# 8 KB transfers and groups in twos in the expert layer of a decoder trunk

## The chip, the cores and the metric

One core of a Trainium2 chip runs the whole program. The metric is the device time of one execution in microseconds (us). TensorE (PE) multiplies matrices into PSUM accumulators, PEld is its weight load, VectorE (DVE) and ScalarE (ACT) do elementwise work, GpSimd (POOL) issues the gathers through index lists, and SyncE (SP) issues the transfers of weights from HBM, which 16 DMA engines carry out.

## The reference, cut to what matters

Two layers over 256 tokens of width 1024, float32. Layer 0 is windowed attention and a dense SwiGLU, layer 1 a Mamba-2 mixer and eight experts, of which each token takes two. The change touches the expert part alone:

```python
logits = (h @ w_router)
top_vals, top_idx = lax.top_k(logits, 2)
top_w = jax.nn.softmax(top_vals, axis=-1)
combine = sum(one_hot(top_idx, 8) * top_w[..., None], axis=-2)
out = 0
for e in range(8):
    g, u = split(h @ w_gu[e], 2)            # w_gu[e]: 1024 x 7168
    out = out + combine[..., e:e + 1] * ((silu(g) * u) @ w_down[e])   # w_down[e]: 3584 x 1024
```

The weights of the eight experts are 352 MB, and all of them are read once.

## The kernel before, in words

A weight tile is 128 rows by 1024 columns (512 KB, 4 KB in each partition). A large matrix product is done in three parts: ScalarE writes a rounded copy of the tile (w_hi, `split_hi`), VectorE the remainder (w_lo, `split_lo`), and TensorE multiplies high by high, high by low and low by high (L2600, L2601, L2608 in `weight_tile`). There are four places each for w_hi and w_lo (SPLIT), so ScalarE can be four tiles ahead of TensorE.

An expert has 84 tiles: seven groups of columns of w_gu, eight tiles (k) each, and 28 tiles of w_down. Groups 0, 2, 4 are gates, group 1 is half gate and half up, 3, 5, 6 are up (`MIX_COLS`, `MIX_UP`). The experts are sorted by their number of tokens and dealt out in pairs: the even one, `p`, has 128 slots and uses the three-part product; the odd one has 64 slots and is multiplied in plain float32 straight from the landed tile (L3097 in `small_step`, no split). `pair_order` writes out the order of tiles (`MOE_SEQ`): in the first pair (r = 0) 16 tiles of the large expert run ahead and then small and large units take turns; in later pairs all 84 large tiles come first and then all 84 small ones.

A large group fills one of two accumulators `acc[0]`, `acc[1]` of 128x1024, in turn (`Body.pair`: `(q + r) % 2` with q = j % 2); the small expert's groups fill the halves of `acc[2]`, and its output goes to the accumulator r % 2. TensorE waits in `open_pair` until the accumulator was emptied. The emptying is `mix_gates` (ScalarE, Silu) and `mix_products` (VectorE), and for an expert's output `output` (VectorE: `yw` or `y_s`, L2026). VectorE and ScalarE run through `MOE_SEQ` in a fixed order: at each tile first the split of that tile, then what `DUE` holds for it. A group's emptying is due three tiles after its last one, an expert's output three tiles after its last.

SP goes through `MOE_LOADS`. 30 tiles of expert 0 are loaded early, into places that come free in the layer before (`FIRST_MOE`, `FIRST_TILES`, `home_free`). Then SP waits for `order_ready`, which says which expert is next, and loads the rest in the order of `MOE_SEQ` into 20 places (12 of `raw` and 8 others, `STAYS`); each load waits until the former tile there was used (L821). Routing is done on VectorE: `positions`, then at given tiles of expert 0 `order_of_experts` (step 4), `second_expert` (6), `rows_of_slots` (18), `places_of_tokens` (21), `positions_of_tokens` (23).

Of the kernel before, what the change touches and what calls it, by code (L numbers as in the profile page):

```python
# [15 lines left out]
P = 128  # L16
# [24 lines left out]
RAW = 12  # L41
# [16 lines left out]
LARGE_AHEAD = 2  # L58
# [34 lines left out]
def build(nc, A, out, square_in, table_in, overflow_at=P):  # L93
# [305 lines left out]

    def units(p):  # L400
        steps = [KD] * FJ + [FK // 4] * 4
        return [[(p, n) for n in range(sum(steps[:u]), sum(steps[:u + 1]))] for u in range(len(steps))]

    def pair_order(r):
# [4 lines left out]
        for u, later in enumerate(small_):  # L409
# [3 lines left out]
    FIRST_MOE = ("row_b", 4, "more0", "more1", "mod5", "mod0", "once0", "once1", "once2", "once3", 5, 6, 7, "mod1",  # L413
                 "once4", "once5", "once6", "once7", 8, 9, 10, 11, 12, 13, 14, 15, "mod2", "mod3", "mod4", "rest8")
    FIRST_TILES = ("row_b", 4, "more0", "more1", "mod5", 5, 6, 7, 8, 9, 10, 11, 12, 13, 14, 15, "once0", "once3", "once7",
                   "mod2", "mod3", "mod4", "rest8", "once4", "once1", "once5", "once2", "once6", "mod0", "mod1")
    ONLY_ONCE = ("mod0", "mod1") + tuple(f"once{n}" for n in range(8))
    STAYS = ("row_b", "more0", "more1", "mod5", "mod2", "mod3", "mod4", "rest8")
    assert len(ONLY_ONCE) == RAW_ONCE and len(STAYS) == RAW_EXTRA
    raw_homes = {n: raw[:, n, :] for n in range(RAW)}  # L420
# [5 lines left out]
    def home_of(what):  # L426
        return (raw0["wout"] + what) % RAW if isinstance(what, int) else RAW + (STAYS + ONLY_ONCE).index(what)
# [5 lines left out]
    SECOND_FROM = len(FIRST_MOE)  # L433
    MOE_LOADS = [(0, FIRST_TILES.index(home)) for home in FIRST_MOE]
    MOE_LOADS += [tile for tile in MOE_SEQ if tile not in MOE_LOADS]
    raw_home, raw_turn, raw_before, turns, held = {}, {}, {}, {}, {}

    def keep_in(no, home):
        turns[home] = turns.get(home, 0) + 1
        raw_home[no], raw_turn[no], raw_before[no] = home, turns[home], held.get(home)  # L440
        held[home] = no

    for no in range(raw0["moe"]):
        keep_in(no, no % RAW)
    free = []
    for m, (p, n) in enumerate(MOE_LOADS):
        no = raw0["moe"] + MOE_AT[p, n]
        if m < len(FIRST_MOE):
            keep_in(no, home_of(FIRST_MOE[m]))
            if FIRST_MOE[m] not in ONLY_ONCE:  # L450
                free.append(raw_home[no])
        else:
            keep_in(no, min(free, key=lambda home: held[home]))
    for n in range(BODY):
        keep_in(raw0["moe"] + EXPERTS * BODY + n, n % RAW)
# [4 lines left out]
    def raw_landed(no):  # L460
        return raw_ready[raw_home[no]], 16 * raw_turn[no]
# [18 lines left out]
    SMALL_SLOT_AT = (35, 51, 59, 61)  # L480
    ORDER_AT, SECOND_AT, SLOTS_AT, PLACES_AT, POS_AT = 4, 6, 18, 21, 23
# [3 lines left out]
    def body_pieces(mixture):  # L485
        after = {}
        for j in range(FJ):
            if mixture:
                gi = MIX_GROUP[j]
                after.setdefault(KD * (gi + 1) + 3 + 2 * MIX_UP[gi].index(j), []).append(("h", j, 0))  # L490
            else:
                after.setdefault(KD * (j + 1) + 3, []).extend(("h", j, t) for t in range(T))
        if mixture:
            for n in range(len(G_BLOCKS)):
                after.setdefault(FJ * KD + 8 + 4 * n, []).append(("gather", n))
# [20 lines left out]
    def round_pieces():  # L516

        n = len(G_BLOCKS)
        for p, step_ in MOE_SEQ:
            found = []  # L520
            if p % 2 == 0:
# [5 lines left out]
                if step_ == (KD * LARGE_AHEAD - 1 if p == 0 else FJ * KD + 8):  # L527
                    found.append(("picked",) if p == 0 else ("small",))
            else:
# [5 lines left out]
                found += [("gather", g) for g in range(len(G_BLOCKS) if p < STORED else 0) if step_ == FJ * KD + 8 + 4 * g]  # L535
# [14 lines left out]
    def events_of_round():  # L550

        due = {}
        for m, (p, step_) in enumerate(MOE_SEQ):
            if step_ < FJ * KD and step_ % KD == KD - 1:
                due.setdefault(m + 3, []).append(("group", p, step_ // KD))
# [157 lines left out]
    class Body:  # L713
# [26 lines left out]
        def pair(self, j, t):  # L740
# [4 lines left out]
            if not self.rnd:  # L745
# [3 lines left out]
                q = (1 if j == FJ else j) % 2  # L749
                return (q + r) % 2, before_pair((q + r) % 2, r) + (3 if j == FJ else j // 2)  # L750
            q = 2 if j == FJ else j % 2
            return q, self.used[q] + (0 if j == FJ else j // 2) + rep(self.e, moe_uses[q])

        def half(self, j):

            return j % 2, self.p // 2 * (4, 3)[j % 2] + j // 2

        def full(self, j):

            return self.spl + KD * (j + 1) + rep(self.e, BODY)  # L760
# [5 lines left out]
    def small_rows(j):  # L766
        return acc[2][:, j % 2 * HALF:(j % 2 + 1) * HALF]
# [28 lines left out]
    def mixture_source(w_gu, w_down, s):  # L796
        if s < FJ * KD:
            gi, k = divmod(s, KD)
            return w_gu[k * P:(k + 1) * P, MIX_COLS[gi]:MIX_COLS[gi] + TW]
        k = s - FJ * KD  # L800
        return w_down[k * P:(k + 1) * P, :]

    block = nc.Block()
    with block:
# [3 lines left out]
        def _(sp):  # L808
            def load(no, src):

                before = raw_before[no]
# [6 lines left out]
                dst = raw_tile(no)  # L818
                if len(src.shape) == 3:
                    dst = dst.rearrange("p (h n) -> p h n", h=src.shape[1])  # L820
                sp.dma_start(dst, src).then_inc(raw_ready[raw_home[no]], 16)  # L821
# [90 lines left out]
            def home_free(m):  # L912

                if m == 0:
                    sp.wait_ge(w_used, spl0["wout"] + 4)
                elif m == 2:
# [3 lines left out]
                elif FIRST_MOE[m] == "mod1":  # L920
                    sp.wait_ge(w_used, spl0["wout"] + 8)
                elif FIRST_MOE[m] == "once4":
                    sp.wait_ge(xb_full, y_piece(3, 1) + 1)
                elif FIRST_MOE[m] == "mod2":
                    sp.wait_ge(gated, gated_no("wout", 2 * KD - 1))
                elif FIRST_MOE[m] == "mod3":
                    sp.wait_ge(hm_rest, 4 * T)
                    sp.wait_ge(hm_rows, T)
                elif FIRST_MOE[m] == "rest8":
# [2449 lines left out]
```

## Time and profile before

| | us |
|---|---|
| median of 3 runs (1513.43 to 1515.9) | 1515.46 |
| the profiled execution, its own time | 1516.27 |
| its span, first to last instruction | 1514.5 |
| TensorE busy | 1463.6 (97%) |
| VectorE busy | 988.8 (65%) |
| ScalarE busy | 746.2 (49%) |
| mean transfer rate over the span | 331 GB/s |
| mean granted TensorE clock | 0.996 |

The span is 1.8 us shorter than the execution's own time. Busy time of TensorE is modelled at its ends, so that 97% is not a statement on its peak. The expert layer begins at 643 us and takes more than half of the time.

### The profile page before, as it was taken

Reading aid. Unit: us, or ns where it says so; the run is one execution under the profiler, and the core shown is the slowest. Engines: PE = TensorE matmul, PEld = TensorE weight load, DVE = VectorE, ACT = ScalarE, POOL = GpSimd, SP = SyncE. Lnnn points to the kernel's source line nnn. Section 1 sums busy time; section 2 is a strip of 40 time slices with the busy share of each in tenths; the row PEclk is TensorE's granted clock in tenths of the full one; section 3 lists DMA queues with packets and bytes.
Section 4 is the critical chain, followed back from the end, with each engine's and each line's share of the span. In section 5 each row is a group of like instructions: output and inputs, shape, how many; then the busy total and the mean of one; then the engine's idle time right before and its main releaser. Section 6 shows DMA issues by size and latency. Waiting matters only on the chain.

```text
span 1514.5 us, 19554 instructions
## 1 busy us (share of the span) xinstructions
PE 1463.6 (97%) x6964; PEld 978.7 (65%) x6964; DVE 988.8 (65%) x1258; ACT 746.2 (49%) x977; POOL 13.8 (1%) x18
## 2 busy tenths in 40 slices
PE   7989999999999999899999999999999998999996
PEld 2836788788789888676666578632678531778431
DVE  2578788888668989776665689611789410989311
ACT  3574544444366876455544577500677300877200
POOL 0000000000000000001000000000000000000000
PEclk9999999999999999999999999999999999999999
DMA  9878698888265337688999999999999999999996
GB/s 363 320 272 287 250 392 308 295 287 305 68 228 167 98 101 262 249 308 329 410 409 409 401 409 408 372 411 400 409 409 409 409 409 399 409 409 408 392 409 266
DMA packets 156947, 501.90 MB, mean 331 GB/s; under 512 B 18483, under 2 KB 21196, under 8 KB 156840
## 3 DMA queue, kind: packets, MB, share of 16 engines
q1 hardware_dynamic: 155560, 496.53, 86.3%
q0 software_dynamic: 1280, 4.01, 0.8%
q8 instruction: 58, 0.95, 0.3%
q14 instruction: 49, 0.40, 0.1%
HBM read 498.33 MB, written 2.29 MB: 331 GB/s over the span
## 4 chain that ended last, share of the span: by engine, by line
PE 83%; DMA 6%; DVE 4%; SPq 3%; ACT 2%; issue 1%; DVEq 0%; ACTq 0%
PE acc L2600 18%; PE acc L2608 17%; PE acc L2601 17%; PE acc L3097 14%; SPq L821 3%; DMA raw<-in_moe_w_down 2%; DVE w_lo L1517 1%; PE xb L2986 1%; PE acc L2749 1%; PE xb L3027 1%; DMA raw<-in_moe_w_gu 1%; DMA raw_more<-in_moe_w_gu 1%; DMA mod<-in_moe_w_down 1%; PE xb L2648 1%; PE acc L3221 1%
## 5 line engine op out<-in xcount | busy, mean ns | idle before, releaser
L1517 DVE TENSOR_TENSOR w_lo<-raw,w_hi 128x1024 fp32r<-128x1024 f32 x353 | 425.6, 1223 | 107.2 <-ACT w_hi L976 97.4
L976 ACT ACTIVATE w_hi<-raw 128x1024 fp32r<-128x1024 f32 x353 | 370.1, 1059 | 200.2 <-PE acc L2608 142.8
L2600 PE MATMUL acc<-w_hi,g_hi 128*128 128x512 f32 x448 | 179.1, 400 | 2.6 <-issue 2.6
L2601 PE MATMUL acc<-w_hi,g_lo 128*128 128x512 f32 x448 | 174.9, 390 | 0.0
L2600 PE MATMUL acc<-w_hi,a_hi 128*128 128x512 f32 x384 | 153.5, 400 | 0.8
L2601 PE MATMUL acc<-w_hi,a_lo 128*128 128x512 f32 x384 | 149.9, 390 | 0.0
L2608 PE MATMUL acc<-w_lo,g_hi 128*128 128x512 f32 x448 | 138.8, 391 | 1.7 <-DVE w_lo L1517 0.9
L3097 PE MATMUL acc<-raw,g_s 128*64 128x512 f32 x552 | 128.2, 597 | 0.0
L2608 PE MATMUL acc<-w_lo,a_hi 128*128 128x512 f32 x384 | 118.4, 390 | 0.0
L2600 PEld LDWEIGHTS acc<-w_hi,g_hi 128*128 128x128 f32 x448 | 84.1, 188 | 34.6 <-issue 15.2
L1517 DVE TENSOR_TENSOR w_lo<-mod,w_hi 128x1024 fp32r<-128x1024 f32 x68 | 82.3, 1222 | 27.0 <-ACT w_hi L976 24.3
L2608 PEld LDWEIGHTS acc<-w_lo,g_hi 128*128 128x128 f32 x448 | 83.7, 188 | 21.9 <-DVE w_lo L1517 3.9
L2601 PEld LDWEIGHTS acc<-w_hi,g_lo 128*128 128x128 f32 x448 | 84.2, 188 | 16.3
L976 ACT ACTIVATE w_hi<-mod 128x1024 fp32r<-128x1024 f32 x68 | 71.6, 1060 | 37.4 <-PE acc L2608 21.4
L3097 PEld LDWEIGHTS acc<-raw,g_s 128*64 128x64 f32 x552 | 37.4, 137 | 75.2 <-issue 74.9
L2600 PE MATMUL acc<-w_hi,e_hi 128*128 128x512 f32 x216 | 85.7, 397 | 0.0
L2600 PEld LDWEIGHTS acc<-w_hi,a_hi 128*128 128x128 f32 x384 | 72.1, 188 | 19.0 <-DVE h L1931 2.8
L2601 PE MATMUL acc<-w_hi,e_lo 128*128 128x512 f32 x216 | 84.2, 390 | 0.0
L2608 PEld LDWEIGHTS acc<-w_lo,a_hi 128*128 128x128 f32 x384 | 72.1, 188 | 15.6
L2601 PEld LDWEIGHTS acc<-w_hi,a_lo 128*128 128x128 f32 x384 | 72.2, 188 | 13.8
L3097 PE MATMUL acc<-raw,e_s 128*64 128x512 f32 x268 | 71.4, 631 | 9.2 <-DMA raw<-in_moe_w_down 8.7
L1975 DVE TENSOR_TENSOR gate<-gate,acc 64x512 f32<-64x512 f32 x28 | 19.2, 684 | 77.4 <-PE acc L3097 72.8
(408 smaller groups left out, 2126.9 us busy)
## 6 DMA issues: line engine op xcount, KB each, us to landing
raw<-in_moe_w_gu SPq DMA_DIRECT2D x263, 512.0 KB, 12.5
raw<-in_moe_w_down SPq DMA_DIRECT2D x135, 512.0 KB, 15.1
raw<-in_ada_w SPq DMA_DIRECT2D x96, 512.0 KB, 5.9
mod<-in_moe_w_gu SPq DMA_DIRECT2D x90, 512.0 KB, 12.8
raw<-in_ffn_w_gu SPq DMA_DIRECT2D x56, 512.0 KB, 5.9
raw_more<-in_moe_w_gu SPq DMA_DIRECT2D x44, 512.0 KB, 12.2
mod<-in_moe_w_down SPq DMA_DIRECT2D x42, 512.0 KB, 15.2
raw<-in_ssm_w_in SPq DMA_DIRECT2D x40, 512.0 KB, 4.7
```

The lines of the kernel that those rows point to most:

```text
L821: sp.dma_start(dst, src).then_inc(raw_ready[raw_home[no]], 16)
L976: act.activation(w_hi[:, w % SPLIT, :], raw_tile(no), ACT.Copy).then_inc(hi_ready, 1)
L1517: dve.tensor_tensor(w_lo[:, w % SPLIT, :], raw_tile(no), r32(w_hi[:, w % SPLIT, :]), ALU.subtract).then_inc(raw_used, 1)
L1975: ins = dve.tensor_tensor(hidden, hidden, small_rows(j)[part, :], ALU.mult)
L2600: pe.matmul(o, l_hi[:, k, rows_], hi[:, col:col + HALF], start=new, stop=False)
L2601: pe.matmul(o, l_lo[:, k, rows_], hi[:, col:col + HALF], start=False, stop=False)
L2608: mm = pe.matmul(o, l_hi[:, k, rows_], lo[:, col:col + HALF], start=False, stop=end)
L2648: mm = pe.transpose(b[:, m * P:(m + 1) * P], src(m), ident)
L2749: mm = pe.matmul(o[j:j + 32, 0:HALF], cond[:, k:k + 1].to_broadcast([P, 32]), raw_tile(no)[:, cols], start=k == 1, stop=k >= KD - 2, skip_ ...
L2986: mm = pe.transpose(b[:, m * P:(m + 1) * P], hidden[:, m * P:(m + 1) * P], ident)
L3027: mm = pe.matmul(b[:, :], put_w[0][:, t, :], yw[:, hf * HALF:(hf + 1) * HALF], start=True, stop=True)
L3097: mm = pe.matmul(rows_[at_:at_ + SMALL, :], lhs[:, k, :], raw_tile(no)[:, m * HALF:(m + 1) * HALF], start=k == 0, stop=last, skip_group_ch ...
```

## The change

Tiles of the expert layer are loaded two at a time by one transfer of 1 MB into two neighbouring places. Where it can be, each partition gets one contiguous run of 8 KB instead of 4. For w_gu that needs two groups whose columns are neighbours, so the groups run in twos: (0, 2), (1, 3), (4), (5, 6), and their tiles alternate; group 4 stays alone, with two rows of 4 KB. For w_down each partition takes two neighbouring rows, so that the order of the hidden columns changes with it (`block_of`: the transposes read every second column). The groups of a two need two accumulators at once. `LARGE_AHEAD` is 1 unit of 16 tiles instead of 2 of 8. `order_of_experts` is done on VectorE before most of the first low parts, cut into two functions; the weights of the tokens and the other routing steps are done later, where the first small tiles run. The table for Silu is loaded before the early splits of ScalarE. Pieces of work (transposes of hidden columns, gathers, slots) have new steps.

```diff
-LARGE_AHEAD = 2
+LARGE_AHEAD = 1
+    GROUP_TWOS = ((0, 2), (1, 3), (4,), (5, 6))
+    GROUP_OF = [(js[n % len(js)], n // len(js)) for js in GROUP_TWOS for n in range(len(js) * KD)]
+    GROUP_OF += [(FJ, k) for k in range(FK)]
+    GROUP_HALF = (0, 0, 1, 1, 0, 1, 0)
+    GROUP_USE = (0, 1, 0, 1, 2, 2, 3)
+    GROUPS_DUE = {GROUP_END[js[0]] + 2: js for js in GROUP_TWOS}
+    HIDDEN_AT = (35, 37, 39, 59, 61, 63, 65)
-        steps = [KD] * FJ + [FK // 4] * 4
+        steps = [2 * KD, 2 * KD, KD, 2 * KD] + ([KD, KD, KD - 2, KD - 2] if p % 2 else [FK // 2, FK // 2])
+    FIRST_LOADS = ((14, "row_b"), (0, "more0", "more1"), (16, "once0", "once1"), (18, "once2", "once3"), (2, 4, 5), (4, 6, 7), (28, "mod0", "mod1"),
+                   (26, "once4", "once5"), (20, "once6", "once7"), (6, 8, 9), (8, 10, 11), (10, 0, 1), (12, 2, 3),
+                   (22, "mod2", "mod3"), (24, "mod4", "mod5"), (15, "rest8"))
-    ORDER_AT, SECOND_AT, SLOTS_AT, PLACES_AT, POS_AT = 4, 6, 18, 21, 23
+    GATHERS_AT = {0: (68, 72, 76), 1: (64, 68, 72)}
+    ORDER_AT, SECOND_AT, SLOTS_AT, PLACES_AT, POS_AT = 19, 10, 17, 18, 19
...
                 r = self.p // 2
                 if self.p % 2:
                     return r % 2, before_pair(r % 2, r) + 4
-                q = (1 if j == FJ else j) % 2
-                return (q + r) % 2, before_pair((q + r) % 2, r) + (3 if j == FJ else j // 2)
+                q = 1 if j == FJ else GROUP_HALF[j]
+                return (q + r) % 2, before_pair((q + r) % 2, r) + (3 if j == FJ else GROUP_USE[j])
...
+    def block_of(m):
+        return slice(m // 2 * 2 * P + m % 2, (m // 2 + 1) * 2 * P, 2)
...
+                elif n < FJ * KD:
+                    gi, k = GROUP_OF[n]
+                    if GROUP_OF[n + 1][0] == gi:
+                        dst = two_tiles(homes[0])
+                        src = w_gu[k * P:(k + 2) * P, MIX_COLS[gi]:MIX_COLS[gi] + TW].rearrange("(h p) n -> p h n", h=2)
+                    else:
+                        dst = two_tiles(homes[0]).rearrange("p h n -> p (h n)")
+                        src = w_gu[k * P:(k + 1) * P, MIX_COLS[gi]:MIX_COLS[gi] + 2 * TW]
+                else:
+                    k = n - FJ * KD
+                    dst = two_tiles(homes[0]).rearrange("p h n -> p (h n)")
+                    src = w_down[k * P:(k + 2) * P, :].rearrange("(p h) n -> p (h n)", h=2)
+                sp.dma_start(dst, src).then_inc(raw_ready[homes[0]], 16)
...
-            early_hi("moe", MOE_BEFORE)
-
             warm(ACT.Silu)
+            early_hi("moe", MOE_BEFORE, 2)
...
             positions()
-            for n in range(len(G_BLOCKS)):
+            gathered_lo(pc0["moe"], 0, highs_moe + 1)
+            early_lo("moe", MOE_BEFORE, 2)
+            order_of_experts()
+            for n in range(1, len(G_BLOCKS)):
                 gathered_lo(pc0["moe"] + n, n, highs_moe + n + 1)
-                if n:
-                    early_lo("moe", n, 2 * n)
+                early_lo("moe", n + 1, n + 2)
             first_round()
```

## Rows read from the trace of the kernel before

**Rows 1.** The page: busy time; transfer rate in 40 slices, GB/s.
```profile
PE 1463.6 (97%) x6964; PEld 978.7 (65%) x6964; DVE 988.8 (65%) x1258; ACT 746.2 (49%) x977; POOL 13.8 (1%) x18
...
GB/s 363 320 272 287 250 392 308 295 287 305 68 228 167 98 101 262 249 308 329 410 409 409 401 409 408 372 411 400 409 409 409 409 409 399 409 409 408 392 409 266
```

**Rows 2.** Windows: length, busy us (instructions), clock, DMA share, GB/s.
```profile
643.00:975.20 332.20, 331.32 (x1488) 225.09 (x1486) 236.08 (x255) 190.97 (x202) 9.34 (x9) 1.00 0.98 386
...
1287.10:1412.30 125.20, 124.44 (x548) 98.44 (x548) 111.81 (x103) 94.04 (x95) 0.00 (x0) 1.00 1.03 409
975.20:1066.60 91.40, 86.86 (x373) 26.21 (x373) 11.47 (x20) 7.76 (x14) 0.91 (x1) 0.98 1.01 394
1191.90:1287.10 95.20, 88.64 (x374) 25.41 (x373) 11.49 (x20) 7.75 (x14) 0.91 (x1) 0.98 1.03 405
1412.30:1504.60 92.30, 86.04 (x365) 24.27 (x364) 9.94 (x17) 5.33 (x10) 0.00 (x0) 1.00 0.95 375
```

**Rows 3.** Timeline, TensorE, two tiles' starts: start us, us.
```profile
1405.48 0.39 PE L2600 MATMUL acc<-w_hi,e_hi 128*128 128x512 f32 x1
...
1406.84 0.39 PE L2600 MATMUL acc<-w_hi,e_hi 128*128 128x512 f32 x1
```

**Rows 4.** Windows, small expert's matmuls (L3097) alone.
```profile
975.20:1036.00 60.80, 54.70 (x246) 16.92 (x248) 1.00 1.00 392
```

**Rows 5.** Timeline of SP's issues in the projection.
```profile
413.71 12.33 SPq L821 DMA_DIRECT2D raw<-in_ssm_w_in  x9
```

**Rows 6.** Windows: the projection (2 KB) and the last small expert (4 KB).
```profile
420.00:424.00 4.00, 4.00 (x20) 3.27 (x19) 3.78 (x7) 3.63 (x5) 0.00 (x0) 1.00 1.06 392
424.00:428.00 4.00, 4.00 (x24) 3.34 (x23) 1.65 (x2) 0.91 (x1) 0.00 (x0) 1.00 1.06 388
1440.00:1455.00 15.00, 15.00 (x68) 4.99 (x68) 2.06 (x3) 1.20 (x2) 0.00 (x0) 1.00 1.03 410
1410.00:1425.00 15.00, 15.00 (x69) 5.85 (x69) 2.34 (x5) 1.37 (x3) 0.00 (x0) 1.00 0.95 364
```

**Rows 7.** Timeline, all engines, start of the expert layer.
```profile
637.40 1.99 ACT L976 ACTIVATE w_hi<-raw_more 128x1024 fp32r<-128x1024 f32 x2
...
639.41 1.28 ACT L990 ACT_TABLE_LOAD   x1
...
640.81 0.85 ACT L1313 ACTIVATE g_hi<-xb 128x512 fp32r<-128x512 f32 x2
...
641.50 1.02 DVE L2064 TENSOR_TENSOR g_lo<-xb,g_hi 128x512 fp32r<-128x512 f32 x2 [0.55 <-ACT g_hi L1313]
...
643.16 0.48 PE L2600 MATMUL acc<-w_hi,g_hi 128*128 128x512 f32 x1
...
649.62 0.36 SPq L821 DMA_DIRECT2D raw_row<-in_moe_w_gu  x1
```

**Rows 8.** Groups by line, 1287 to 1413: busy us, mean ns, idle before.
```profile
L1517 DVE TENSOR_TENSOR w_lo<-raw,w_hi 128x1024 fp32r<-128x1024 f32 x51 | 61.3, 1223 | 23.0 <-ACT w_hi L976 21.4
L976 ACT ACTIVATE w_hi<-raw 128x1024 fp32r<-128x1024 f32 x50 | 52.6, 1060 | 12.8 <-PE acc L2608 11.4 <-DMA raw<-in_moe_w_gu 1.3
...
L1211 ACT ACTIVATE gate_l<-acc 128x1024 f32<-128x1024 f32 x3 | 3.1, 1020 | 0.5 <-PE acc L2608 0.5
...
L2083 DVE TENSOR_TENSOR gate_l<-gate_l,acc 128x512 f32<-128x512 f32 x4 | 2.6, 680 | 0.0
...
L1214 ACT ACTIVATE gate_end<-acc 128x512 f32<-128x512 f32 x1 | 0.6, 600 | 0.3 <-PE acc L2608 0.3
```

**Rows 9.** Timeline, all engines, a turn from small to large.
```profile
1065.46 1.06 ACT L976 ACTIVATE w_hi<-mod 128x1024 fp32r<-128x1024 f32 x1 [14.79 <-DMA mod<-in_moe_w_gu]
...
1066.62 0.47 PE L2600 MATMUL acc<-w_hi,g_hi 128*128 128x512 f32 x1 [1.34 <-issue]
...
1070.26 1.41 DVE L2026 TENSOR_TENSOR y_s<-acc,mod 64x512 f32<-64x512 f32 x2
...
1072.98 0.50 PE L2608 MATMUL acc<-w_lo,g_hi 128*128 128x512 f32 x1 [0.73 <-DVE w_lo L1517]
```

More of the change, by code:

```diff
@@ L426, in home_of, with two_tiles @@
     def home_of(what):
-        return (raw0["wout"] + what) % RAW if isinstance(what, int) else RAW + (STAYS + ONLY_ONCE).index(what)
+        return what if isinstance(what, int) else RAW + (STAYS + ONLY_ONCE).index(what)
+    def two_tiles(a):
+        if a < RAW:
+            return raw[:, a:a + 2, :]
+        name = (STAYS + ONLY_ONCE)[a - RAW]
+        at_ = int(name[-1])
+        return (mod if name[:3] == "mod" else raw_more if name[:4] == "more" else raw_once)[:, at_:at_ + 2, :]
     MOE_SEQ = [tile for r in range(EXPERTS // 2) for tile in pair_order(r)]
@@ L432, in build @@
         natives.append(natives[-1] + p % 2)
[L433 to L453, printed above, removed]
+    raw_home, raw_sem, raw_turn, turns, held = {}, {}, {}, {}, {}
+    def keep_in(nos, homes):
+        before = max((held[home] for home in homes if home in held), default=None)
+        turns[homes[0]] = turns.get(homes[0], 0) + 1
+        for no, home in zip(nos, homes):
+            raw_home[no], raw_sem[no], raw_turn[no] = home, homes[0], turns[homes[0]]
+            held[home] = no
+        return before
@@ new lines, in build, with moe_load @@
+    raw_before = {no: keep_in([no], [no % RAW]) for no in range(raw0["moe"])}
+    MOE_LOADS = []
+    def moe_load(tiles, homes):
+        nos = [raw0["moe"] + MOE_AT[tile] for tile in tiles]
+        MOE_LOADS.append((tiles, nos, homes, keep_in(nos, homes)))
+    for n, *names in FIRST_LOADS:
+        moe_load([(0, n + m) for m in range(len(names))], [home_of(name) for name in names])
+    SECOND_FROM = len(MOE_LOADS)
+    FIRST_TILES = sum(len(names) for _, *names in FIRST_LOADS)
+    homes_of_two = [(n, n + 1) for n in range(0, RAW + RAW_EXTRA, 2)]
@@ L454, in build @@
+    for m, (p, n) in enumerate(MOE_SEQ):
+        if n % 2 == 0 and (p or n >= FIRST_TILES):
+            homes = min(homes_of_two, key=lambda two: max(held[two[0]], held[two[1]]))
+            if homes[0] == RAW:
+                for q in range(2):
+                    moe_load([(p, n + q)], [homes[q]])
+            else:
+                moe_load([(p, n), (p, n + 1)], list(homes))
     for n in range(BODY):
-        keep_in(raw0["moe"] + EXPERTS * BODY + n, n % RAW)
+        raw_before[raw0["moe"] + EXPERTS * BODY + n] = keep_in([raw0["moe"] + EXPERTS * BODY + n], [n % RAW])
@@ L494, in body_pieces @@
             for n in range(len(G_BLOCKS)):
-                after.setdefault(FJ * KD + 8 + 4 * n, []).append(("gather", n))
+                after.setdefault(GATHERS_AT[0][n], []).append(("gather", n))
         else:
@@ L534, in round_pieces @@
                     found.append(("add", p - 1, ADDS_AT[p > 1].index(step_)))
-                found += [("gather", g) for g in range(len(G_BLOCKS) if p < STORED else 0) if step_ == FJ * KD + 8 + 4 * g]
+                found += [("gather", g) for g in range(len(G_BLOCKS) if p < STORED else 0) if step_ == GATHERS_AT[1][g]]
             for what in found:
@@ L553, in events_of_round @@
         for m, (p, step_) in enumerate(MOE_SEQ):
-            if step_ < FJ * KD and step_ % KD == KD - 1:
-                due.setdefault(m + 3, []).append(("group", p, step_ // KD))
+            if step_ + 1 in GROUP_END.values() and step_ < FJ * KD:
+                j = GROUP_OF[step_][0]
+                at_ = next(at_ for at_, js in GROUPS_DUE.items() if j in js)
+                due.setdefault(m + at_ - step_, []).append(("group", p, j))
             if step_ == BODY - 1 and p < STORED:
@@ L1923, in body @@
                         split_lo(B.raw_no(s), B.spl + s, e)
+                    for gi in GROUPS_DUE.get(s, ()) if B.mixture else ():
+                        mix_products(B, gi)
                     j, k = divmod(s, KD)
-                    if 1 <= j <= FJ and k == 2:
-                        if B.mixture:
-                            mix_products(B, j - 1)
-                        for t in range(0 if B.mixture else T):
+                    if not B.mixture and 1 <= j <= FJ and k == 2:
+                        for t in range(T):
                             q, _ = B.pair(j - 1, t)
```

140 lines of the change are left out of this document (73 added, 67 removed).

## The prediction

> **What bounds the kernel now.** I read the page first: TensorE is busy for 97% of the span, and from about slice 19 of 40 on the transfers run at 409 GB/s [rows 1]. Both look full, so the page alone cannot say which one sets the end. The windows by stretch can [rows 2]. The expert layer is one large expert (128 slots, PE work 1.36 us a weight tile: two tile starts lie 1406.84 - 1405.48 apart [rows 3]) and one small expert (64 slots) in turn. Up to 975.2 us TensorE is never idle (331.3 of 332.2 us). Then come small 91.4, large about 125, small 95.2, large 125.2, small 92.3 us. In the large stretches TensorE works 124.4 of 125.2 us: they are set by TensorE. In the small stretches it idles 4.5, 6.6 and 6.3 us while the transfers run near their full rate: there the transfers decide. The small stretch's own floor is the start at 975.2 us, where 246 matmuls, 61.5 tiles, took 60.8 us out of full buffers [rows 4], so about 1.0 us a tile with its other work, 84 us in all. So faster transfers can shorten three stretches of some 92 us, by at most some 8 us each, and nothing else.
>
> **Transfers of 8 KB.** A tile is 524,288 bytes. At 410 GB/s (pieces of 4 KB) it takes 1.280 us; in the projection, where SP issues ssm_w_in in pieces of 2 KB, the queue runs as full and moves 392 and 388 GB/s [rows 5, 6]. With the latter, a piece takes one of the 16 engines 84.5 ns at 2 KB (2,048 x 16 / 388) and 159.8 ns at 4 KB, so 75.3 ns for 2 KB more; a straight line gives 310.4 ns for 8 KB, 422 GB/s. With 392 it is 420. I take 420, 1.248 us a tile, a gain of 0.032. Bounds: 409 (an 8 KB piece costs two of 4 KB) and 435 (the slope of 75.3 ns alone, the fixed part of 9 ns gone). The Trainium skill (DMA: Bandwidth & Descriptors, "Why small descriptors are slow (HBM only)") gives a fixed overhead of about 3 cycles a packet beside one cycle per 32 bytes: 262 cycles against 259 for 8 KB, 1.1%. By it the gain would be 0.014 us a tile and the small stretches would come out some 3 us worse in total than below; the trace's step from 2 to 4 KB is about twice what that rule gives, so I go by the rows.
>
> In a small stretch of the new kernel 20 tiles are there at its start, since the buffers fill in the large stretch before it. Counting tiles by GB/s x time, the old stretches moved 68.7, 73.5 and 66.0 tiles [rows 2]; the second was longer because its buffers weren't full at its start. In the new kernel I count 69.7 for the first two (one more, because the large expert starts on a pair) and 64 for the last. Group 4 stays at 4 KB, 8 tiles. 61.7 x 1.248 + 8 x 1.280 = 87.2 us. To this comes the restart of the queue: the first free buffer is now a pair, so two tiles of 0.9 us plus 1.6 us until data flow, 3.4 us. In all 90.6: -0.8 and -4.6 us. The last stretch: 64 tiles are 56 x 1.248 + 8 x 1.280 = 80.1, the restart 3.4, what its old time holds beside 66.0 tiles of 84.5 and 1.7 of queue idle at its start (15 x (1 - 364 / 410) [rows 6]) is 6.1, and 0.9 comes on top because the last two tiles come together and are worked off one after the other: 90.5, -1.8 us. **Small stretches -7.2 us.**
>
> **The start.** ScalarE does two splits (1.99 us) and the table load (1.28) before the gather's high part at 640.81; VectorE's low part at 641.50 waits for it [rows 7]. The change leaves one split there, and takes six VectorE operations of 0.2 us from ahead of positions. The first gather piece is ready from about 639.7, so the high part starts 1.1 us earlier, the third piece's transposes follow, and the first expert tile starts at 642 instead of 643.16: **-1.2 us**; this carries to 975.2, since TensorE doesn't wait in between. The order of the experts is ready at about 643, so SP goes on at 644 instead of 649.62. I cost this at nothing: TensorE has 30 tiles in store and needs none of these transfers; buffers come free only as it works (1.36 us a tile), and at 975 us the buffers are full either way. Its cover would be gone if the 16 small tiles at 669 us were late; they are loaded by 663. second_expert (four VectorE operations and two picks, 1 us) at tile 10 is due at 655 and needed at 664; rows, places and positions lie in VectorE's slack beside the first small tiles.
>
> **Groups in twos hold TensorE.** A large expert's accumulators are two. Before, eight tiles fill one while the other is emptied; now tiles alternate between both, and a new pair of groups opens both within two tiles. Three places:
>
> (1) At a tile 56 (down) the accumulator of group 5 is needed, whose last tile is 54. VectorE first does the low part of tile 57 (its high part needs tile 53 done), then two products of 0.68. From tile 53's end: 0.3 + 1.06 + 1.22 + 1.3 = 3.9 us; TensorE is there at 2.72: 1.1 us lost. At tile 32 group 1's accumulator waits for Silu 0.60, the low part of 33 and a product 0.68: 0.5 us. At 17 and 41 only a Silu of 1.02 stands in the way, under one tile's 1.36: nothing [rows 8]. 1.6 x 3 large stretches (in the first pair of experts small tiles lie between): **+4.8 us**.
>
> (2) The turn from small to large is what I think decides. The small expert's output sits in the accumulator that the next large expert's group 2 takes. The first group to take it was group 1, at tile 8; now it is group 2, at tile 1. VectorE empties it (y_s, 1.41 us) only after the low part of the third large tile: 1070.26, 3.6 us after TensorE's first tile [rows 9]. That cost nothing at tile 8. Now tile 1 waits for it: from the landing of the first pair, the third tile lands 2.5 us later, high 1.06 + 0.2, low 1.23, y_s 1.41: 6.5 us; TensorE wanted it at 2.7. Lost 3.8, less 0.7 that it lost there before anyway (it waited for a low part, the last of [rows 9]): 3.1 us at each of two turns. At the first turn, near 851 us, tiles are in store and VectorE's three low parts follow the last add, at small tile 80 (1.1 on TensorE, 0.7 on VectorE): 1.8 + 3 x 1.15 + 1.4 = 6.7 against 1.1 + 3 x 0.88 + 1.36 = 5.0: 1.7. **+7.9 us**, and the large stretches are TensorE's, so it isn't made good; the transfers only fill the buffers sooner.
>
> (3) In the small expert the same alternation stands behind transfers, so nothing.
>
> **Strided transposes** for the new row order: 28 x 4 per large expert of 0.1 us; between nothing and double, +3 us a stretch; the address step alone gives no reason, I take nothing.
>
> Sum: -7.2 - 1.2 + 4.8 + 7.9 = **+4.3 us** on the profiled 1516.27 (span 1514.5 and 1.8 around it): 1520.6. The median of the runs is 0.8 below the profiled one: 1519.8, +0.28%.
>
> **The rivals.** (a) Forecast, chance 0.50, own range 1515 to 1524 (the waits of (1) and (2) by a third either way). (b) TensorE isn't held: the accumulators come free in time, so 12.7 us fall away: 1507.1. For it: VectorE is busy only 112 of 125 us in a large stretch. Against: its order is fixed by program, and [rows 9] show it. It is faster than before by a measurable amount as soon as (1) and (2) together cost less than 5.3 us. Chance 0.22. (c) 8 KB pieces move no faster than 4 KB: 61.7 x 0.032 x 3 = 5.9 more, 1525.7. For it: no row shows a piece above 4 KB. Chance 0.14. The skill's page on DMA (section "SWDGE vs HWDGE vs iDMA") calls packets of up to 4096 B the preferred ones, which would go with this; nothing here shows it. (d) They move at 430: (1.248 - 1.219) x 61.7 x 3 = 5.4 less, 1514.4. Chance 0.14.
>
> About 0.2% (3 us) is what a measurement can tell from no change: 1512.4 and 1518.5. Faster: (b) 0.20, (d) 0.03, (a) 0.01: 0.24. Same: (a) 0.15, (d) 0.11, (b) 0.02: 0.28. Slower: (a) 0.34, (c) 0.14: 0.48. Range 1506 to 1527: from just below (b) to just above (c).
>
> **What would show it.** GB/s near 420 in small stretches (right), 409 (c). TensorE's second large tile starts 5 us after its first at two turns and the wait names y_s (2). Waits before tiles 32 and 56 in each large stretch, which grow from 125 to about 130 us. First expert tile at 642. Queue idle at all large stretches' ends. I am wrong if VectorE's y_s comes ahead of the third low part, or if a large stretch stays at 125 us.

## The result and the profile after

The changed kernel takes 1528.06 us (median of 4 runs, 1527.55 to 1529.39), the kernel before 1515.68 (1513.43 to 1516.59); the ratio is 1.0084, 95% interval 1.0072 to 1.0097. It is **slower by 12.4 us**, where 4.3 were forecast, and lies just above the range of 1506 to 1527. The profiled execution took 1529.39 us, its span is 1527.6; so the two profiles stand 13.1 us apart. No time below counts one execution, of the kernel with the gates later, that took 2441 us at a mean granted clock of 0.56.

The page of the changed kernel, against [rows 1]: busy time, transfer rate in 40 slices, and the number of transfer pieces.

```profile
PE 1464.9 (96%) x6964; PEld 989.8 (65%) x6964; DVE 990.2 (65%) x1258; ACT 745.4 (49%) x977; POOL 16.1 (1%) x18
...
GB/s 362 316 277 285 243 393 310 288 287 310 75 214 157 106 101 295 219 329 295 419 420 419 409 409 346 356 417 408 420 416 369 376 418 409 418 413 334 377 418 304
DMA packets 117017, 501.79 MB, mean 328 GB/s; under 512 B 13635, under 2 KB 16348, under 8 KB 81848
```

Work is the same (6964 matmuls), the rate has risen from 409 to 419 and 420 where the queue is full, and yet other slices fell to 334 to 377. These lie mostly where a large stretch ends: the buffers are full there and SP waits for one to come free (106 and 107 us in sum in the last two large stretches, 36 in the last one before). TensorE is busy in them (18.9 of 18.9 us from 1165.0 on, at 326 GB/s): it takes a tile every 1.36 us, less than the queue can bring. The windows by stretch, against [rows 2], cut at the first matmul of each kind (length, busy of TensorE, its weight loads, VectorE, ScalarE, GpSimd, granted clock, DMA share, GB/s):

```profile
669.96:685.54 15.58, 15.58 (x65) 4.89 (x65) 4.51 (x15) 2.43 (x3) 0.00 (x0) 0.89 0.70 269
685.54:711.49 25.95, 22.84 (x100) 17.95 (x98) 21.02 (x37) 16.49 (x18) 9.79 (x7) 1.00 0.72 277
...
856.00:983.54 127.54, 125.09 (x551) 98.85 (x549) 110.66 (x102) 90.65 (x92) 0.96 (x1) 1.00 0.99 384
983.54:1075.04 91.50, 84.82 (x373) 26.86 (x373) 11.48 (x20) 7.85 (x15) 0.91 (x1) 1.00 0.99 401
1075.04:1206.13 131.09, 127.19 (x548) 99.99 (x548) 112.78 (x103) 93.42 (x95) 0.96 (x1) 0.97 0.99 399
1206.13:1297.09 90.96, 84.67 (x374) 26.79 (x373) 11.49 (x20) 7.85 (x15) 0.91 (x1) 1.00 1.00 404
1297.09:1429.66 132.57, 128.18 (x548) 100.83 (x548) 112.66 (x103) 93.50 (x95) 0.00 (x0) 0.97 0.99 389
1429.66:1519.15 89.49, 83.77 (x365) 25.92 (x364) 9.88 (x16) 5.33 (x10) 0.00 (x0) 1.00 0.95 385
```

In the kernel before the same cuts give 91.41, 125.27, 95.21, 125.27 and 92.13 us from 975.21 on. So the two later small stretches are 4.3 and 2.6 us shorter, the first one is not, and the large ones are 5.8 and 7.3 us longer, not 4.7. In the first three windows stands what the prediction had not seen at all: the first small stretch begins at 983.54 instead of 975.21. The waits of TensorE from 643 to 985 and from 985 to 1510 us (us in total, times, longest):

```profile
PE acc L2669 <- DVE w_lo L1569: 3.1, 2, 2.7
PE acc L2661 <- ACT w_hi L1028: 1.3, 1, 1.3
PE acc L2661 <- DVE gate_l L2136: 1.0, 1, 1.0
...
PE acc L3157 <- DMA raw<-in_moe_w_down: 8.0, 9, 2.2
PE acc L2661 <- DVE y_s L2078: 5.9, 2, 3.2
```

y_s and gate_l are the forecast holds (2) and (1); a hold is idle time of TensorE because an accumulator isn't emptied yet or a part isn't ready. The first row is not forecast: TensorE waits for low parts, at 691 and 695 us. The timeline there, all engines:

```profile
684.79 0.60 ACT L1313 ACTIVATE gate<-acc 128x512 f32<-128x512 f32 x1 [13.00 <-PE acc L3157]
...
685.65 0.60 ACT L1313 ACTIVATE gate<-acc 128x512 f32<-128x512 f32 x1 [0.26 <-PE acc L3157]
...
686.15 3.89 ACT L1028 ACTIVATE w_hi<-raw_once 128x1024 fp32r<-128x1024 f32 x4
...
687.31 1.23 DVE L1569 TENSOR_TENSOR w_lo<-raw_once,w_hi 128x1024 fp32r<-128x1024 f32 x1 [11.51 <-ACT w_hi L1028]
...
688.45 0.38 DVE L2223 TENSOR_TENSOR chosen<-oh,row_at 128x16 f32<-128x16 f32 x2
...
689.98 1.23 DVE L1569 TENSOR_TENSOR w_lo<-raw_once,w_hi 128x1024 fp32r<-128x1024 f32 x1
...
691.12 0.16 DVE L2174 TENSOR_TENSOR cnt<-cnt,cap 128x8 f32<-128x8 f32 x1
...
694.05 0.22 DVE L2052 TENSOR_REDUCE comb_pos<-at_pos 128x8 f32<-128x64 f32 x1
694.30 2.36 DVE L1569 TENSOR_TENSOR w_lo<-raw_once,w_hi 128x1024 fp32r<-128x1024 f32 x2
...
695.58 0.73 PE L2669 MATMUL acc<-w_lo,g_hi 128*128 128x512 f32 x2 [2.66 <-DVE w_lo L1569]
```

ScalarE has the gates of the first small expert's groups 0 and 2 in its order ahead of the high parts of large tiles 18 and 19. In twos, both gates are ready only when all 16 small tiles are done (before, the first was ready after eight). ScalarE stands for 13.00 us, the high parts start at 686.15, and VectorE, idle for 11.51 us, gets its low parts only when TensorE already works on the large tiles. Between them lie places (from 688.45) and then the count of slots and the positions (691.12 to 694.27). In the 11.5 us just before there had been room for all of it.

The turn at 1075 us, against [rows 9]:

```profile
1075.04 0.47 PE L2661 MATMUL acc<-w_hi,g_hi 128*128 128x512 f32 x1 [1.68 <-issue]
...
1076.25 1.22 PE L2669 MATMUL acc<-w_lo,g_hi 128*128 128x512 f32 x2
...
1078.62 1.40 DVE L2078 TENSOR_TENSOR y_s<-acc,mod 64x512 f32<-64x512 f32 x2
...
1080.17 0.76 PE L2661 MATMUL acc<-w_hi,g_hi 128*128 128x512 f32 x1 [2.70 <-DVE y_s L2078]
...
1082.01 1.05 PE L2669 MATMUL acc<-w_lo,g_hi 128*128 128x512 f32 x2
```

The wait for y_s is there at 2.70 us (3.18 at the other turn). But the second tile's low products follow the first's by 5.76 us, not by 1.36 + 2.70: the remaining 1.70 is the clock. A matmul of 0.40 us takes 0.63 here, and the first behind the wait 0.76. Windows over these places:

```profile
670.10:673.50 3.40, 3.40 (x10) 0.95 (x10) 2.59 (x4) 1.69 (x2) 0.00 (x0) 0.50 0.00 1
1076.30:1083.10 6.80, 4.10 (x9) 2.83 (x10) 5.91 (x6) 2.95 (x3) 0.00 (x0) 0.50 1.02 422
1301.60:1308.40 6.80, 6.19 (x15) 4.87 (x16) 4.05 (x4) 2.06 (x3) 0.00 (x0) 0.50 1.02 423
```

The granted clock is 0.50 in them (1.2 of 2.4 GHz). At both turns TensorE had worked with gaps of 0.4 to 2.2 us between pairs at the end of the small stretch. At the first the clock fell at 1076.3, ahead of the wait of 2.70 us (from 1077.5 on); at the other at 1301.6, within the wait of 3.18. What TensorE works at half clock behind the waits differs too: 2.93 us (to 1083.1) and 6.11 us (to 1308.3), so that 1.5 and 3.1 us are lost. The kernel before has such a stretch too, but of 3.4 us, at 1058 and at 1280 us, where TensorE waits for transfers in any case and loses little by it.

### The profile page after: what moved, and what is told of

Its sections match the earlier page's. It is cut to its first block, busy times and chain, and to the rows that moved or that the text cites. A ratio compares the mean times of both kernels' runs of the same rounds, so it can differ in the third digit from the quotient of the medians.

```text
span 1527.6 us, 18720 instructions
## 1 busy us (share of the span) xinstructions
PE 1464.9 (96%) x6964; PEld 989.8 (65%) x6964; DVE 990.2 (65%) x1258; ACT 745.4 (49%) x977; POOL 16.1 (1%) x18
## 3 DMA queue, kind: packets, MB, share of 16 engines
q0 software_dynamic: 1280, 4.01, 0.8%
## 4 chain that ended last, share of the span: by engine, by line
PE 86%; DMA 7%; DVE 4%; ACT 2%; issue 1%; SPq 0%; DVEq 0%; ACTq 0%
PE acc L2661 18%; PE acc L2669 17%; PE acc L2662 17%; PE acc L3157 16%; DMA raw<-in_moe_w_gu 2%; DMA raw_more<-in_moe_w_gu 1%; DMA raw<-in_moe_w_down 1%; PE xb L3047 1%; PE acc L2810 1%; PE xb L3088 1%; DVE w_lo L1569 1%; PE xb L2709 1%; DMA raw<-in_ada_w 1%; DMA raw_more<-in_moe_w_down 1%; PE acc L3281 1%
## 5 line engine op out<-in xcount | busy, mean ns | idle before, releaser
L1028 ACT ACTIVATE w_hi<-raw 128x1024 fp32r<-128x1024 f32 x350 | 365.9, 1058 | 233.1 <-PE acc L2669 164.8
L3157 PE MATMUL acc<-raw,e_s 128*64 128x512 f32 x280 | 67.5, 603 | 9.2 <-DMA raw<-in_moe_w_down 9.1
```

The costliest lines, as they stand in the source:

```text
L1028: act.activation(w_hi[:, w % SPLIT, :], raw_tile(no), ACT.Copy).then_inc(hi_ready, 1)
L3157: mm = pe.matmul(rows_[at_:at_ + SMALL, :], lhs[:, k, :], raw_tile(no)[:, m * HALF:(m + 1) * HALF], start=k == 0, stop=last, skip_group_ch ...
```

## The experiments

Each edit is made on the changed kernel. The ratio is to the kernel before on the same chip, with its 95% interval, from 4 to 12 runs. TensorE's first expert tile moves by up to 2.7 us between kernels that don't differ ahead of it, in step with where the half-clock stretches of the stages before lie (figures in the last section); the lengths of single stretches are free of that.

**y_s earlier.** The output of a small expert is emptied behind the first low part of the next large expert, not the third.

```
-                due.setdefault(m + 3, []).append(("out", p))
+                due.setdefault(m + (1 if p % 2 else 3), []).append(("out", p))
```

> The changed kernel, but VectorE empties a small expert's output (y_s) right behind the low part of the next large expert's first tile, not behind that of its third. Theory (the turn costs both its wait and TensorE's clock behind it): the waits of 2.70 and about 3 us for y_s at the second large tile go, and with them the stretches of granted clock 0.5 behind them, 3.4 us longer each than those of the kernel before, so some 1.7 us of work each; with 1.3 us at the first turn the time falls by 8 to 10 us, to about 1519, and the windows of 15 us at the turns show a granted clock above 0.9. Rival A (the clock falls for another reason, the late first pair of the small stretch's end): only the waits go, 5 to 6 us, about 1522.5, clock as in the changed kernel. Rival B (the low part of the second large tile, now behind y_s, becomes the one that is late): 1.4 of each wait comes back, the gain is 3 us or less, 1525.

Measured: 1518.9 us, ratio 1.0032 (1.0021 to 1.0044): 0.0052 less than the changed kernel, 7.9 us. Waits after 985 us, and windows over two half-clock stretches and both large stretches:

```profile
PE acc L2661 <- DVE y_s L2078: 1.1, 2, 0.7
```

```profile
1064.50:1067.90 3.40, 3.39 (x8) 1.01 (x10) 0.00 (x0) 0.00 (x0) 0.00 (x0) 0.51 1.01 413
1074.70:1078.10 3.40, 2.97 (x8) 1.86 (x7) 3.33 (x5) 2.77 (x3) 0.00 (x0) 0.50 1.02 423
1073.16:1201.49 128.33, 126.69 (x549) 99.59 (x549) 112.46 (x103) 93.41 (x95) 0.96 (x1) 0.99 1.01 406
1292.73:1420.32 127.59, 125.70 (x548) 98.72 (x549) 112.04 (x103) 93.42 (x95) 0.00 (x0) 1.00 1.00 404
```

The waits fall from 5.9 to 1.1 us, and the large stretches from 131.1 and 132.6 to 128.3 and 127.6. That is 7.8 us for 4.8 us of waits; the other 3.0 is clock (1.5 and 3.1 us lost before, 1.5 now), so rival A, by which only the waits go, falls. Rival B falls too, since no wait for a low part appears. At one turn, however, a half-clock stretch of 3.4 us is still there at 1074.7, behind a wait of 0.43 us, with another ahead of it at 1064.5: the wait for y_s makes the clock's fall longer and more costly, but isn't its only cause.

**Products of groups 5 and 6 one tile earlier.**

```
-    GROUPS_DUE = {GROUP_END[js[0]] + 2: js for js in GROUP_TWOS}
+    GROUPS_DUE = {GROUP_END[js[0]] + (1 if js[0] == 5 else 2): js for js in GROUP_TWOS}
```

> The changed kernel, but the products of groups 5 and 6 stand one tile earlier in VectorE's order, ahead of the low part of tile 57. Theory (the accumulator of group 5 holds tile 56): the wait of 1.0 us for gate_l at tile 56 goes in each of the four large experts, 3 to 4 us in all, about 1524.5, with no new wait. Rival A (the low part of tile 57 is late in its place, since both products of 0.68 us and the wait for tile 55 stand ahead of it): the wait moves to tile 57, nothing gained, 1528. Rival B (part of the hold is recovered in the small stretches by fuller buffers): 1 to 2 us.

Measured: 1526.54 us, ratio 1.0076 (1.0061 to 1.0091). The difference to 1.0084 is inside the intervals. The profile is clearer: the three waits of 1.0 us for gate_l are gone, and there were three, not four, because in the first expert small tiles lie between. There the edit adds a wait of its own, at tile 57 of the first expert:

```profile
780.17 2.80 DVE L2027 TENSOR_TENSOR gate<-gate,acc 64x512 f32<-64x512 f32 x4 [2.55 <-PE acc L3157]
...
784.17 0.73 PE L2669 MATMUL acc<-w_lo,e_hi 128*128 128x512 f32 x2 [0.69 <-DVE w_lo L1569]
```

These are the low parts of tile 57, the second large tile behind 16 small ones, and what stands ahead of them on VectorE are the products of the small expert's groups 5 and 6, which the same edit moved. So some 2 us net, by the profile alone; rivals A and B can't be told from the theory by the time.

**The first small expert's gates later.** ScalarE does them behind the high parts of large tiles 18 and 19. VectorE's order is untouched.

```
-                due.setdefault(m + at_ - step_, []).append(("group", p, j))
+                due.setdefault(m + at_ - step_ + (2 if (p, j) in ((1, 0), (1, 2)) else 0), []).append(("group", p, j))
```

> The changed kernel, but ScalarE does the first small expert's two gates behind the high parts of large tiles 18 and 19, not ahead of them; VectorE's routing steps stay behind the low parts of tiles 17, 18 and 19. Theory (ScalarE's order makes the high parts 12 us late, and only so do places and positions come to lie on the path): the high and low parts of 18 and 19 and the routing steps are done while TensorE works the 16 small tiles, the holds of 0.45 and 2.66 us at 686 to 696 us go, 3.5 to 4 us gained, about 1524. Rival A (the routing steps are on the path wherever VectorE's low parts run behind): nothing gained, a hold of the same size at tile 20 or 21. Rival B (most of the 8.3 us by which the first stretch is longer lies elsewhere, in the start and the clock): the holds go, but the second round's first tile moves by less than 2 us.

**Routing steps later.** ScalarE's order is untouched.

```
-    ORDER_AT, SECOND_AT, SLOTS_AT, PLACES_AT, POS_AT = 19, 10, 17, 18, 19
+    ORDER_AT, SECOND_AT, SLOTS_AT, PLACES_AT, POS_AT = 24, 10, 17, 20, 22
```

> The changed kernel, but with VectorE's routing steps later: places behind the low part of tile 20, positions behind that of 22, the count of slots behind that of 24; ScalarE's order as it is. Theory (the steps hurt because they stand between late low parts; a little later VectorE has no store of low parts either, since it works 1.23 of each tile's 1.36 us): the 3.9 us of steps still cost TensorE most of their length, 0 to 1.5 us gained, about 1527. Rival (they hurt only where they stand, between tiles 18 and 20): 3.5 us gained, 1524.5.

Measured: 1523.32 us, 1.0047 (1.0030 to 1.0064) with the gates later; 1524.51 us, 1.0073 (1.0053 to 1.0092) with the steps later. Windows from the first large tile behind the 16 small ones to the next small tile, first with the gates later:

```profile
682.65:704.91 22.26, 22.26 (x101) 18.12 (x99) 15.66 (x15) 14.88 (x16) 4.42 (x4) 1.00 0.87 333
```

and with the steps later:

```profile
681.12:706.24 25.12, 23.46 (x101) 17.81 (x99) 20.94 (x37) 16.49 (x18) 9.02 (x7) 1.00 0.70 261
```

In the changed kernel this window is 25.95 us. With the gates later it is 22.26, TensorE busy throughout, and VectorE has 15 instructions in it instead of 37: the rest has moved to where it was idle. With the steps later it is 25.12: 2.9 of the 3.7 us stay. So it isn't the place of the steps but ScalarE's order that puts them on the path. Rival A of the first and the rival of the second fall, by these windows: in time alone the second edit can't be told from the changed kernel (1.0073 against 1.0084, runs from 1522.9 to 1531.3). With the gates later the ratio fell by 0.0037, 5.6 us, more than the 3.7: the profile of the changed kernel, and those of the two edits before, have a half-clock stretch of 3.4 us ahead of the hold or in it (1.7 us of work), and here there is none; nor is there one with the steps later. One profile each cannot show that the hold causes it.

**All three together** (the products of groups 5 and 6 earlier in all but the first large expert).

> Three reorderings in one on the changed kernel: y_s right behind the first low part of the next large expert, the products of groups 5 and 6 one tile earlier (not in the first expert), the first small expert's gates behind the high parts of large tiles 18 and 19. Theory (the holds are separate and add up): from the changed kernel's 1.0084 of the kernel before, 0.0052 for the first, some 0.0015 for the second and 0.0037 for the third go: 0.998, some 1511.5 where the kernel before takes 1514.3; TensorE's idle time from the first expert tile on falls from 35 us to about 24 us. Rival (a hold that goes lets the next one come to the front, or the small stretches take back what the large ones give): half of the 15 us at most, 1.001, 1516.

Measured: 1512.99 us, ratio 1.0000 (0.9990 to 1.0011), and TensorE's idle times from the first expert tile to the end of the last small stretch sum to 23.1 us instead of 33.2. The three edits alone took 0.0052, 0.0008 and 0.0037, which would leave 0.9987; the difference to 1.0000 is no larger than the intervals. So the holds are separate and mostly add up; the 0.998 expected was 3 us too good. By the time alone the rival's 1.001 isn't excluded; what speaks against it are the 10 us of idle time that went, while the three small stretches took back 0.8 us in sum (272.7 against 272.0). The wait of 0.7 us at tile 57 of the first expert is still there (at 777.5), since the first small expert's products are earlier here too. Windows of its large stretches, and TensorE's waits in the first of them:

```profile
1067.67:1194.45 126.78, 125.82 (x548) 98.64 (x548) 111.86 (x103) 93.37 (x95) 0.96 (x1) 1.00 1.01 409
...
1285.75:1412.56 126.81, 125.84 (x548) 98.65 (x549) 111.72 (x103) 93.38 (x95) 0.00 (x0) 1.00 1.01 406
```

```profile
PE acc L2661 <- issue: 1.7, 1, 1.7
PE acc L2661 <- DVE y_s L2078: 0.7, 1, 0.7
```

Each is still 1.5 us longer than 125.27. The rest of the wait for y_s, 0.7, is no more than the 0.73 that TensorE lost at this turn before [rows 9]. Tile 32 starts 0.3 us late and tile 56 0.3, and the transposes take some 0.2 us more; the rest, 0.7, I can't name.

**Pieces of 4 KB.** A pair is loaded by two DMAs of 512 KB into the same buffers; order and buffers are the same, but the number of DMAs doubles for these pairs.

```
-        turns[homes[0]] = turns.get(homes[0], 0) + 1
+        turns[homes[0]] = turns.get(homes[0], 0) + len(homes)
...
-                sp.dma_start(dst, src).then_inc(raw_ready[homes[0]], 16)
+                if len(tiles) == 1:
+                    sp.dma_start(dst, src).then_inc(raw_ready[homes[0]], 16)
+                for q in range(len(tiles) if len(tiles) == 2 else 0):
+                    sp.dma_start(raw_tile(nos[q]), mixture_source(w_gu, w_down, n + q)).then_inc(raw_ready[homes[0]], 16)
```

> The changed kernel, but each pair of tiles is loaded by two DMAs of 512 KB in pieces of 4 KB into the same pair of buffers, which still counts as landed when both are there; order and buffers are as in the changed kernel. Theory (the larger piece is worth its rate, 409 to 410 against 420 GB/s, in the three small stretches alone): each small stretch is about 2 us longer, 5 to 6 us in all, 1533.5, ratio 1.012; the large stretches stay as they are. Rival (the shorter small stretches of the changed kernel come from fuller buffers at their start, the piece size matters nothing): 1528, no change. Further rival (a first 4 KB tile of a pair lands earlier and shortens the waits at the turns): this can't show, since both tiles wait for the whole pair.

> The three reorderings with the 4 KB pieces of the run before. Theory (where TensorE isn't held, the piece size is still worth about 2 us in each of three small stretches): 5 to 6 us above the three reorderings with 8 KB pieces, about 1517, ratio 1.002. Rival (without the holds TensorE comes earlier into the small stretches, and the buffers have had less time to fill, so the rate decides more): 8 us or more above.

Measured: on the changed kernel 1535.55 us, ratio 1.0143 (1.0129 to 1.0158), 9 us more than with 8 KB. On the three reorderings 1520.14 us, ratio 1.0039 (1.0026 to 1.0052), 5.9 us more. Windows of the small stretches with 4 KB on the changed kernel:

```profile
980.91:1075.41 94.50, 87.02 (x373) 26.75 (x373) 11.49 (x20) 7.84 (x15) 0.90 (x1) 0.98 1.01 393
1206.74:1299.86 93.12, 86.62 (x373) 27.07 (x373) 11.49 (x20) 7.84 (x15) 0.90 (x1) 0.98 1.02 398
1431.25:1523.15 91.90, 83.96 (x365) 25.73 (x364) 9.89 (x16) 5.33 (x10) 0.00 (x0) 1.00 0.96 377
```

They are 3.0, 2.2 and 2.4 us longer than with 8 KB, 7.6 in sum; 6 were forecast. The piece's size matters by its rate: where the queue is full, the page reads 409 again. That it isn't the number of DMAs shows in the next version, where the large experts' gate and up tiles come in DMAs of 1 MB with 4 KB pieces: their queue moves 410 GB/s too (first line), where the changed kernel has 423 in such a short window (second line).

```profile
1078.00:1084.00 6.00, 6.00 (x29) 4.95 (x28) 5.10 (x6) 5.19 (x7) 0.00 (x0) 1.00 1.03 410
...
1084.00:1090.00 6.00, 6.00 (x28) 4.99 (x27) 5.09 (x5) 4.48 (x5) 0.00 (x0) 1.00 1.02 423
```

**Twos in the small experts alone.** The tables of groups are made once for large and once for small experts: a large expert's groups come singly, as in the kernel before (its down tiles stay 8 KB), a small one's in twos. The gates of the first small expert are later, as above. y_s and all products stay where the change has them.

```
+    GROUP_TWOS = (tuple((j,) for j in range(FJ)), ((0, 2), (1, 3), (4,), (5, 6)))
+    GROUP_HALF = ((0, 1, 0, 1, 0, 1, 0), (0, 0, 1, 1, 0, 1, 0))
+    GROUP_USE = ((0, 0, 1, 1, 2, 2, 3), (0, 1, 0, 1, 2, 2, 3))
...
-                    if B.mixture and s in (0, KD, KD + 4):
-                        n = max(s // 4 - 1, 0)
+                    if B.mixture and s in (0, 4, 6):
+                        n = max(s // 2 - 1, 0)
```

> The changed kernel with twos in the small experts alone: a large expert's groups come singly again (its gate and up tiles in pieces of 4 KB, its down tiles in 8 KB), so that TensorE changes its accumulator every eight tiles; the first small expert's gates stand behind the high parts of large tiles 18 and 19. Theory (all that a small stretch loads is a small expert's tiles, so it keeps its whole gain, and the waits at tiles 1, 32 and 56 exist only because of the large expert's twos): large stretches of 125.3 us as in the kernel before instead of 131 to 132.6, small ones of 91.5, 91 and 89 us; about 6 to 8 us faster than the kernel before, 1507, ratio 0.995. Rival (pieces of 4 KB in the large stretches leave the buffers less full when a small stretch starts, or slots of two tiles come free in a worse order): small stretches near 93 to 95 us, ratio 0.999 to 1.001.

> The kernel of the run before (twos in the small experts alone), with each pair loaded by two DMAs of 512 KB in 4 KB pieces. Theory (the gain of the run before is the piece's rate): 6 to 7 us slower than that run, 0.000 to 0.001 above the kernel before in ratio, 1514.5. Rival (its gain is that of the start, the gates and the order of the loads): less than 3 us slower than that run.

Measured: **1508.45 us, ratio 0.9952 (0.9938 to 0.9965)**, and with 4 KB pieces 1515.31 us, 1.0005 (0.9996 to 1.0014). The version with twos in the small experts alone beats both kernels; with 4 KB pieces nothing of the gain is left. Its windows from 972.56 us on:

```profile
972.56:1065.13 92.57, 86.31 (x374) 27.08 (x373) 11.48 (x20) 7.85 (x15) 0.90 (x1) 0.98 1.00 403
1065.13:1191.27 126.14, 126.09 (x549) 100.28 (x549) 111.97 (x103) 93.62 (x95) 0.96 (x1) 0.99 1.02 412
1191.27:1282.82 91.55, 86.08 (x373) 27.27 (x373) 11.48 (x20) 7.84 (x15) 0.90 (x1) 0.98 1.00 404
1282.82:1408.40 125.58, 124.78 (x548) 99.05 (x548) 111.94 (x103) 93.28 (x95) 0.00 (x0) 1.00 1.02 410
1408.40:1497.96 89.56, 83.77 (x365) 25.91 (x364) 9.88 (x16) 5.32 (x10) 0.00 (x0) 1.00 0.94 384
```

Large stretches are back at 126.1 and 125.6 us. The small ones keep most of their gain: they are 1.1, 0.6 and 0.1 us longer than in the changed kernel, so that the first is also 1.2 longer than before. The timeline of the turn shows y_s behind the third low part again, with nobody waiting for it; yet the granted clock is at its lower level here too for some 3.4 us, from 1066.7 on:

```profile
1068.77 1.40 DVE L2078 TENSOR_TENSOR y_s<-acc,mod 64x512 f32<-64x512 f32 x2
```

## Why the prediction was wrong

It had the direction and the two mechanisms it put on TensorE's path, mis-sized the second by leaving out the clock, and missed a third. Its terms against the cuts of the two profiled executions:

| stretch | forecast, us | measured, us |
|---|---|---|
| stages before the experts | 0 | +1.15 |
| start of the expert layer | -1.2 | -0.6 |
| first pair of experts, interleaved | 0 | +4.1 |
| first large expert by itself | +3.3 | +3.7 |
| the two others | +9.4 | +13.1 |
| three small stretches | -7.2 | -6.8 |
| end, behind the last small tile | 0 | -1.5 |
| sum | +4.3 | +13.1 |

**The step that failed** is in the part on the start: "rows, places and positions lie in VectorE's slack beside the first small tiles". I had looked for slack on VectorE and not asked what VectorE waits for there. Its low parts wait for ScalarE's high parts, and ScalarE's order was changed by the same edit: with groups in twos both gates of the first small expert come due behind its last tile, ahead of two high parts. That made VectorE's slack useless, 11.5 us of it, and put 4.5 us of routing steps between low parts that were already late. The run with the gates later gives back 3.7 us of hold in the profile and 5.6 in the time; moving the steps alone gives back 0.8. With the hold gone this pair of experts takes 206.90 us up to the first large expert by itself, against 208.16 before: so the +4.1 is 3.7 of hold and 1.7 of clock at 670 us, less 1.3.

**Groups in twos, (1).** Right in mechanism. Tile 56 starts 1.65 us behind the low products of tile 55, where other tiles start 0.45 behind: 1.2 late (forecast 1.1). Tile 32 is 0.3 late (0.5).

**The turn, (2).** Right in mechanism and place: waits of 2.70 and 3.18 us, y_s behind the third low part. Mis-sized is the price of each turn, 3.1 forecast: up to the sixth large tile the two turns cost 3.8 and 5.2 us. The hold by itself was less than forecast (the second tile starts 3.3 us later than before, where TensorE then lost 1.0 elsewhere: 2.3), but the clock was left out: TensorE comes out of the wait at 0.50 and works 2.93 and 6.11 us like that, which costs 1.5 and 3.1. The large stretches are 5.8 and 7.3 us longer instead of 4.7; with y_s earlier they lose 2.8 and 5.0 again. At the first turn (1.7 forecast; its sum of 5.0 is 5.1) the second tile starts 2.94 us behind the first, 1.6 more than 1.36. The profile puts that wait, 1.29 us, down to a high part that ended at 858.81; but y_s ended at 858.79, the high part is that of a tile four further on, and with y_s earlier the wait is gone.

**Transfers of 8 KB.** Right. The straight line gave 422 and I took 420; the page shows 419 and 420 in slices of 38 us, so 8,192 x 16 / 420 = 312 ns a piece against 310 from the line. Rivals (c) and (d) fall. The Trainium skill (DMA: Bandwidth & Descriptors, "Why small descriptors are slow (HBM only)") names a fixed overhead of about 3 cycles a packet; an estimate from it gives 1.1% for 4 to 8 KB. Measured is 409 to 419 or 420, 2.4 to 2.7%, so here the measurement decides against it. The preference for packets of up to 4096 B, which the prediction took from the Trainium skill (DMA: Bandwidth & Descriptors, "SWDGE vs HWDGE vs iDMA"), stands there in the part on descriptors that GpSimd writes; these transfers are issued by SP, so no run here tests it. The small stretches: forecast -0.8, -4.6, -1.8, measured +0.1, -4.3, -2.6; the total is within 0.4 us, its parts are off by up to 0.9. By their ratios the three pairs of runs value the piece at 5.9, 8.0 and 8.9 us, so rival (c) was priced at 5.9, if anything too low.

**The start.** Half right. From GpSimd's store of hm to the first expert tile it is 10.98 to 11.03 us in all ten kernels with the change and 11.60 before: -0.6, not -1.2. The first split left the path, as said, but ScalarE's second split now stands between the gather's first and second high part. The other 1.15 us lies in stages ahead of that, and varies between the profiled executions.

**Small experts, (3).** Nothing was forecast for their twos. The profile has one wait of 0.5 to 0.6 us for a product in each small stretch (1.6 us in sum, none before), but behind it TensorE waits for transfers in any case, so right in the sum and not in the reason.

**Strided transposes.** Right: 24 of 280 ns instead of 271 in a large stretch, 0.2 us.

**Rival (b)**, TensorE not held, is close to what the version with twos in the small experts alone realizes: 8.4 us below before by forecast, measured 7.2 (1508.45 where the kernel before takes 1514.51). For that the twos didn't have to go everywhere: most of what a small stretch loads, 64 of about 70 tiles by the prediction's count, is the small expert's, and there the twos hold up nobody for more than 0.6 us.

**What stays open.** The end behind the last small tile is 1.5 us shorter (the four output stores issue in 2.51 us instead of 4.30 on SP); no run took it apart. What makes the clock fall at a turn, and for how long, isn't settled: with all three reorderings it doesn't fall there at all in the profiled execution, with y_s alone earlier it falls twice around one turn, for 3.4 us each, and with twos in the small experts alone twice too, though TensorE doesn't wait for y_s. Of the 1.5 us that each large stretch keeps with the three reorderings about half is unnamed.

## What to carry over

Slack on an engine is room only if what it waits for is there: before work is put into it, follow the wait upstream to the engine that feeds it, and see whether the same edit changes that engine's order. When accumulators are filled in turns of two, everything that empties one must be asked for its place again, and a layout change that helps only transfer-bound stretches should be made only for the tiles loaded there. A wait of TensorE of about 3 us on the path was followed here by 1.5 and 3.1 us more that the half clock cost, so that a hold's price isn't its wait alone.

## What the runs showed of the hardware

- Pieces of 8 KB were moved at 419 to 420 GB/s over slices of 38 us, of 4 KB at 409 to 410, of 2 KB at 388 to 392 (windows of 4 us), by the same 16 engines; the steps fit a fixed 9 ns and 75 ns for every 2 KB.
- Around waits of 2.70 and 3.18 us the granted clock was 0.50 for 6.8 us. That isn't fixed: with the same waits but the routing steps later it was 3.4 us at a time, with waits of 0.4 to 0.7 us 3.4 us or nothing, and with no wait for y_s still 3.4 us at one turn. A matmul of 0.40 us took 0.63 there. Behind the two long waits TensorE worked 2.93 and 6.11 us at that clock, and lost half of that.
- The start of the expert layer moved by up to 2.7 us between the profiled executions of versions that don't differ ahead of it, in step with their half-clock stretches of 3.4 us or more: with one near 16 us alone the first expert tile came at 641.0 to 641.5, with one near 82 instead at 642.5 to 642.7, with one near 154 besides at 642.0 (behind one near 16) and 643.7 (behind one near 82). No run was made to test that.
